# Expert weights fetched in runs of 8 KB, with the channels and rows of each expert dealt to the partitions in another way

## The chip, the cores and the metric

The kernel runs on one core of one Trainium2 chip. The metric is the time of one execution in microseconds (us) on the device: the median of three runs, with their lowest and highest. A profiled execution of the same program gives the trace. Its time includes what lies before the first and after the last instruction; its span does not.

## What is computed

One layer of a decoder trunk for 320 tokens (256 of a prompt, 64 of eight sampled sequences), 1024 channels wide: three mixers, then a mixture of experts, then a gated embedding, and a last norm. The change touches only the mixture of experts, cut here to its core:

```python
g_logits = (t @ w_rg).astype(F32) + b_rg.astype(F32)          # 4 groups
e_logits = jnp.einsum('td,dge->tge', t, w_re) + b_re          # 4 experts in each
...                                                           # best group, two best experts in it
hg = jnp.einsum('td,edf->tef', t, w_gate)                     # 16 experts: 1024 -> 512
hu = jnp.einsum('td,edf->tef', t, w_up)                       #             1024 -> 512
act = jax.nn.silu(hg) * hu * combine[..., None].astype(t.dtype)
return jnp.einsum('tef,efd->td', act, w_down).reshape(b, L, d)  #           512 -> 1024
```

All weights are float32: per expert 2 MB for gate, 2 MB for up and 2 MB for down, 16 experts.

## The kernel before

It is written by hand, engine by engine, with semaphores; the order of each engine's instructions is the order of the code. Before the experts the kernel does the mixers and the router. If no expert has more tokens than the plan holds (the case that runs, `crowded` is 0), the experts are worked on in "sorted" form.

**Tokens are gathered by matmuls.** PE turns the normed activations `h` (channels on partitions) to rows of tokens in six pieces of 512 channels (L2013; `h_bank`, six PSUM banks). ACT copies each piece as float32r into `h_hi` (L961, the copy itself is recorded at the helper's line L683). DVE subtracts: `h_lo` = piece − `h_hi` (`h_rest`, L1407 to 1412), so that `h_hi` + `h_lo` is the full value. For each chunk `c` of 128 channels, `gather` (L2035 to 2047) multiplies `h_hi[:, b, c*128:(c+1)*128]`, and then `h_lo`, by a matrix of zeros and ones `pick_t` (made by DVE, L1453). The product is `h_exp`: 128 channels on partitions, one column for each token's place at an expert.

On ACT the six copies stand ahead of the two exponentials of the router (L964, L966), and DVE's router chain waits for these (L1394). On DVE the six subtractions are spread through the rest of that chain: two before L1419, one before L1429, one before L1433, two before the first `pick_t`. SP waits for `crowded_ready` (L1439) before it fetches the first expert.

**Work goes by items.** There are 4 turns of 5 items, 16 experts in 20 items: 13 items hold 64 places, 7 hold 32. `item_groups(n)`, called `g`, is 2 or 4: an item of 64 places uses the PE array as 2 column tiles of 64, an item of 32 places as 4 tiles of 32. For each of the 8 chunks `k` of 128 channels, tile `p` takes its share of the expert's 512 gate and 512 up columns (L2099 to L2101):

```python
for p in range(g):
    m = MM(bank[0][per * p:per * (p + 1), 0:2 * DE // g], h_exp[i % 2][:, k, first_place(n):first_place(n) + per],
           w_gu[u][:, :, k, DE // g * p:DE // g * (p + 1)], start=k == 0, stop=k == DC - 1)
```

ACT takes the silu (L985), DVE multiplies (`act_s`, L1491), PE turns the product to channels on partitions (L2109), DVE copies it (`act_ft`, L1494), and PE multiplies it with the down weights (L2120, four chunks `k`). The result goes back to the tokens' columns by `scatter` (L2064), which PE does between the chunks of the next item's L2100, as it does the next turn's gathers (L2044, L2046) in the waits around L2109. DVE adds it to `x` (L1477).

**Weights are fetched by SP** in `sorted_experts` (L473 to L492) into two buffers `u`. For each expert SP issues gate and up in halves of four chunks (L485, semaphore `gu_loaded{u}{half}`) and down in one transfer (L489). The gate and up of expert `q` wait for `gu_done` of expert `q-2`, its down for `down_done` of expert `q-2`. PE waits for the first half at `k == 0`, for the second at `k == 4` (L2098), and for down before L2120. After the last expert SP fetches `w_ple_gate` (L471) for the next stage (L2166).

In memory the weights of an expert are rows of 512 (gate, up: 2 KB) or 1024 values (down: 4 KB). In the kernel before, chunk `k` on partition `p` is row `128k + p`, so every partition's piece of a transfer is made of separate rows of 2 or 4 KB.

Of the kernel before, what the change touches and what calls it, by code (L numbers as in the profile page):

```python
# [13 lines left out]
P = 128  # L14
# [33 lines left out]
def build(nc, a, o):  # L48
# [80 lines left out]
    with ExitStack() as ctx:  # L129
# [143 lines left out]
        w_down = [weights[:, u, GU:GU + DOWN].rearrange("p (k n) -> p k n", n=D) for u in range(2)]  # L273
        NI = 4 * CAP + CAP // 2
        h_hi, h_lo = in_place("h_hi", "gates", 0, [P, 3, D]), in_place("h_lo", "gates", 3 * D, [P, 3, D])
        pick_t = in_place("pick_t", "gates", 6 * D, [P, 3, NI])
        silu_s = in_place("silu_s", "gates", 6 * D + 3 * NI, [P, DE // 2], F32)
        act_s = in_place("act_s", "gates", 6 * D + 3 * NI + DE // 2, [P, DE // 2], F32)
# [60 lines left out]
        def _(sp):  # L339
# [133 lines left out]
            def sorted_experts():  # L473


                for q in range(NE):
                    u, item = q % 2, ITEMS * (q // 4) + (0, 1, 2, 4)[q % 4]
                    e = sp.value_load(ids[0:1, item:item + 1], min_val=0, max_val=NE - 1)
                    done = ITEMS * ((q - 2) // 4) + (2, 3, 4, 5)[(q - 2) % 4]
                    if q >= 2:  # L480
                        sp.wait_ge(s("gu_done"), done)
                    for hf in range(2):
                        ks = slice(hf * DC // 2, (hf + 1) * DC // 2)
                        for r, w in enumerate(("w_expert_gate", "w_expert_up")):
                            sp.dma_start(w_gu[u][:, r, ks, :], a[w][0][bass.ds(e, 1)].rearrange(  # L485
                                "e (k p) n -> p (e k) n", p=P)[:, ks, :]).then_inc(s(f"gu_loaded{u}{hf}"), 16)
                    if q >= 2:
                        sp.wait_ge(s("down_done"), done)
                    sp.dma_start(w_down[u], a["w_expert_down"][0][bass.ds(e, 1)].rearrange("e (k p) n -> p (e k) n", p=P)  # L489
                                 ).then_inc(s(f"down_loaded{u}"), 16)  # L490
                sp.wait_ge(s("gu_done"), N_ITEMS - 1)
                ple_gate()  # L492
# [157 lines left out]
        def _(act):  # L650
# [307 lines left out]
            for n_ in range(6):  # L958
                n = BLK[n_ // 2][1]
                act.wait_ge(s("h_tok_turned"), n_ + 1)  # L960
                copy(h_hi[0:n, n_ // 2, 512 * (n_ % 2):512 * (n_ % 2) + 512], h_bank[n_][0:n, :]  # L961
                     ).then_inc(s("h_hi_ready"), 1)
            act.wait_ge(s("router_arg"), 1)
            F(R["gexp"], R["gexp"], ACT.Exp).then_inc(s("router_exp"), 1)  # L964
            act.wait_ge(s("router_arg"), 2)
# [54 lines left out]
        def _(dve):  # L1020
# [385 lines left out]

            def h_rest(n_):  # L1407

                n, f = BLK[n_ // 2][1], slice(512 * (n_ % 2), 512 * (n_ % 2) + 512)
                dve.wait_ge(s("h_hi_ready"), n_ + 1)  # L1410
                TT(h_lo[0:n, n_ // 2, f], h_bank[n_][0:n, :], h_hi[0:n, n_ // 2, f].bitcast(F32), ALU.subtract
                   ).then_inc(s("h_lo_ready"), 1)

            dve.wait_ge(s("moe_const"), 2)
            for n_ in range(2):
# [137 lines left out]
        def _(pe):  # L1553
# [477 lines left out]
            with pe.If(pe.value_load(crowded[:, :], min_val=0, max_val=1) == 0):  # L2031
# [3 lines left out]
                def gather(i, c):  # L2035
# [10 lines left out]
                        m = MM(gather_bank(i, c)[:, 0:ni], h_lo[:, b, f], pick_t[:, b, 0:ni], start=False, stop=b == 2)  # L2046
                    m.then_inc(s("gathered"), 1)

                def scatter(n, half):

                    pe.wait_ge(s("y_lo_ready"), n + 1)
                    pe.wait_ge(s("home_ready"), n + 1)
                    g = item_groups(n)
                    per, js = P // g, DC // g
                    for j in range(js // 2 * half, js // 2 * (half + 1)):
                        done = DC * n + j * g
                        if n == N_ITEMS - 1 and half:
                            pe.wait_ge(s("moe_added"), j * g + g - 4)
                        elif done >= 4:
                            pe.wait_ge(s("down_added"), done + g - 4)  # L2060
                        for y_part in (y_hi, y_lo):
                            for q in range(g):
                                rows_ = slice(per * q, per * (q + 1))
                                m = MM(bank[4 + (j * g + q) % 4][:, 0:T], y_part[rows_, j * P:(j + 1) * P], home_s[rows_, n % 2, :],  # L2064
                                       start=y_part is y_hi, stop=y_part is y_lo)
                                if y_part is y_lo:
                                    m.then_inc(s("spread_done"), 1)
# [19 lines left out]
                for n in range(N_ITEMS):  # L2087
# [8 lines left out]
                    for k in range(DC):  # L2096
                        if k % 4 == 0:
                            pe.wait_ge(s(f"gu_loaded{u}{k // 4}"), 32 * (q // 2 + 1))  # L2098
                        for p in range(g):  # L2099
                            m = MM(bank[0][per * p:per * (p + 1), 0:2 * DE // g], h_exp[i % 2][:, k, first_place(n):first_place(n) + per],  # L2100
                                   w_gu[u][:, :, k, DE // g * p:DE // g * (p + 1)], start=k == 0, stop=k == DC - 1)  # L2101
                        if n and k in (2, 5):
                            scatter(n - 1, k // 5)
                    m.then_inc(s("gu_done"), 1)
# [1 line left out]
                        gather(i + 1, 2 * t)  # L2106
                    pe.wait_ge(s("act_ready"), n + 1)
                    for k in range(4 // g):
                        m = TR(bank[1][:, k * P:(k + 1) * P], act_s[:, k * P:(k + 1) * P], ident[:, :])  # L2109
                    m.then_inc(s("act_turned"), 1)  # L2110
                    if ahead:
                        gather(i + 1, 2 * t + 1)
# [109 lines left out]
```

## Time and profile before

| | us |
|---|---|
| median of 3 runs | 948.44 (947.17 to 950.31) |
| profiled execution, whole | 952.26 |
| its span, first to last instruction | 950.5 |
| PE busy in the span | 864.5 (91%) |
| DVE busy | 408.4 (43%) |
| ACT busy | 213.9 (23%) |
| stage of the experts, start of the first L2100 to start of the last L2120 | 629.4 to 887.7 |

The stage of the experts is some 260 us of the span. A line number is that of the kernel before; copies by ACT's helper all carry L683 and are told apart by their tiles. A float32 matmul leaves two records in the trace, one for each pass, so that 16 matmuls of L2100 read as x32. Where two or four column tiles work side by side, a record's own duration is longer than the distance to the next; distances between groups are what counts.

### The profile page before, as it was taken

The numbers are of one execution on the slowest core, as the hardware profiler recorded it, in microseconds if no ns is written. First come the engines' busy times: TensorE is split into PE (matmuls) and PEld (weight loads), VectorE is DVE, ScalarE is ACT, GpSimd is POOL, SyncE is SP. The second block draws the span as 40 slices with busy tenths as digits, with TensorE's granted clock in tenths as the row PEclk, the third lists the DMA queues.
The fourth block names the chain that finished last, engine by engine and source line by source line (L and its number), as shares of the span: only waits on it lengthen the run. The fifth ranks groups of instructions, "written<-read, shape, count | busy, mean of one in ns | idle before, by whom it ended". The sixth has DMA issues, their size and how long they took to land.

```text
span 950.5 us, 12272 instructions
## 1 busy us (share of the span) xinstructions
PE 864.5 (91%) x4535; PEld 525.2 (55%) x4535; DVE 408.4 (43%) x976; ACT 213.9 (23%) x424; POOL 131.4 (14%) x243
## 2 busy tenths in 40 slices
PE   6699999998689969999989999599999999999695
PEld 4377666765466645756547676564444444433473
DVE  3306664556565243333313413513354453454543
ACT  0211434323232232223250012120111111100233
POOL 4002069998000000000000020000000000000000
PEclk9799999999889979999999999689999999999897
DMA  9323312324852526778673100099999999999601
GB/s 264 91 89 109 137 50 88 111 89 151 274 151 52 176 83 219 223 227 263 227 291 115 44 1 1 0 373 348 396 391 349 391 396 381 395 387 396 225 0 56
DMA packets 108366, 190.36 MB, mean 200 GB/s; under 512 B 9001, under 2 KB 33897, under 8 KB 108295
## 3 DMA queue, kind: packets, MB, share of 16 engines
q1 hardware_dynamic: 103120, 184.40, 54.9%
q0 software_dynamic: 1600, 4.34, 1.6%
q10 hardware_dynamic: 3583, 0.80, 0.5%
q8 instruction: 38, 0.62, 0.3%
q14 instruction: 25, 0.20, 0.1%
HBM read 184.23 MB, written 5.64 MB: 200 GB/s over the span
## 4 chain that ended last, share of the span: by engine, by line
PE 68%; POOL 11%; DVE 8%; ACT 3%; issue 3%; ACTq 3%; SPq 3%; DMA 2%; DVEq 0%; POOLq 0%
PE bank L2100 12%; PE bank L1794 9%; POOL ring L597 7%; PE bank L1621 7%; PE bank L2120 6%; PE bank L1963 6%; PE bank L2166 4%; PE bank L1975 4%; PE bank L2064 3%; POOL proj L600 3%; PE bank L1907 2%; PE bank L1859 2%; PE bank L1877 2%; DMA gate_w<-in_w_in 1%; PE bank L2044 1%
## 5 line engine op out<-in xcount | busy, mean ns | idle before, releaser
L1621 PE MATMUL bank<-scratch,ring 128*128 128x320 f32 x512 | 144.5, 439 | 0.0
L2100 PE MATMUL bank<-weights,h_exp 128*64 128x512 f32 (+1 forms) x864 | 125.6, 488 | 1.2 <-issue 1.2
L1794 PE MATMUL bank<-scratch,gate_w 128*128 128x320 f32 x384 | 114.3, 453 | 11.0 <-DMA gate_w<-in_w_in 10.2
L1621 PEld LDWEIGHTS bank<-scratch,ring 128*128 128x128 f32 x512 | 96.5, 192 | 43.1 <-issue 5.5
L1794 PEld LDWEIGHTS bank<-scratch,gate_w 128*128 128x128 f32 x384 | 74.8, 200 | 44.2 <-DMA gate_w<-in_w_in 11.7
L1477 DVE TENSOR_TENSOR x<-x,bank 128x320 f32<-128x320 f32 x160 | 67.3, 482 | 52.4 <-PE bank L2064 52.4
L2100 PEld LDWEIGHTS bank<-weights,h_exp 128*64 128x64 f32 (+1 forms) x864 | 39.9, 122 | 64.2 <-issue 58.2
L597 POOL TENSOR_SCALAR ring<-scratch,par_w 128x64 f32<-128x64 f32 x120 | 68.8, 600 | 2.9
L2120 PE MATMUL bank<-weights,act_ft 128*64 128x512 f32 (+1 forms) x432 | 61.0, 486 | 0.4 <-DVE act_ft L1494 0.4
L1091 DVE SCALAR_TENSOR_TENSOR proj<-scratch,par_w,proj 128x256 f32<-128x256 f32 x120 | 53.5, 510 | 0.2
L621 POOL MEMSET h_hi<- 64x1024 f32 x1 | 0.9, 946 | 302.3 <-DVE proj L1356 302.3
L683 ACT ACTIVATE gates<-bank 128x320 f32<-128x320 f32 (+3 forms) x38 | 17.5, 477 | 104.1 <-PE bank L1794 99.5
L1859 PE MATMUL bank<-ident,ring 128*128 128x128 f32 x256 | 32.2, 284 | 9.6 <-DVE proj L1269 4.8
L2166 PE MATMUL bank<-scratch,ring 128*128 128x320 f32 x128 | 37.7, 456 | 3.5 <-issue 3.5
L718 ACT ACTIVATE proj<-bank 128x320 f32<-128x320 f32 x32 | 14.0, 436 | 114.9 <-PE bank L1621 114.9
L985 ACT ACTIVATE silu_s<-bank 128x256 f32<-128x256 f32 (+1 forms) x20 | 6.9, 346 | 137.9 <-PE bank L2100 137.9
L1963 PE MATMUL bank<-proj,ring 128*128 128x320 f32 x128 | 36.4, 448 | 1.7 <-DVE att L1309 1.7
L1859 PEld LDWEIGHTS bank<-ident,ring 128*128 128x128 f32 x256 | 29.3, 146 | 14.2 <-DVE proj L1269 5.7
L2120 PEld LDWEIGHTS bank<-weights,act_ft 128*64 128x64 f32 (+1 forms) x432 | 20.3, 122 | 30.1 <-issue 24.6
L1975 PE MATMUL bank<-proj,ring 128*128 128x320 f32 x128 | 35.6, 434 | 1.1 <-DVE proj L1356 1.1
L1269 DVE COPY proj<-bank 128x512 f32<-128x512 f32 x32 | 21.5, 689 | 32.8 <-PE bank L1859 32.5
L1498 DVE TENSOR_TENSOR y_lo<-bank,y_hi 128x512 fp32r<-128x512 f32 (+1 forms) x20 | 12.0, 598 | 50.6 <-ACT y_hi L683 50.6
(354 smaller groups left out, 1128.2 us busy)
## 6 DMA issues: line engine op xcount, KB each, us to landing
weights<-in_w_expert_gate SPq DMA_DIRECT2D x32, 1024.0 KB, 11.0
weights<-in_w_expert_up SPq DMA_DIRECT2D x32, 1024.0 KB, 13.2
weights<-in_w_expert_down SPq DMA_DIRECT2D x16, 2048.0 KB, 16.5
ring<-in_w_in SPq DMA_DIRECT2D x8, 2048.0 KB, 7.7
ring<-in_cache_k SPq DMA_DIRECT2D x64, 256.0 KB, 3.9
ring<-in_cache_v SPq DMA_DIRECT2D x64, 256.0 KB, 3.9
gate_w<-in_w_in SPq DMA_DIRECT2D x24, 512.0 KB, 6.5
ring<-in_w_branch SPq DMA_DIRECT2D x3, 2048.0 KB, 8.8
```

Of the source, the lines that this page charges most:

```text
L597: ch.add(pool.tensor_scalar(tap[:, c, :].rearrange("p (b t) -> p b t", b=NB), src, w, None, ALU.mult))
L600: ch(pool.tensor_tensor(proj[:, TA:TA + WC, SEQ:T], proj[:, TA:TA + WC, SEQ:T], tap, ALU.add))
L1091: ch.add(STT(out, src, w, out, ALU.mult, ALU.add))
L1477: TT(x[:, c, :], x[:, c, :], bank[4 + j % 4][:, 0:T], ALU.add).then_inc(s(name), 1)
L1621: m = MM(bank[b_][:, 0:T], slot(j, DC, GROUP)[:, k, (n % 4) * P:(n % 4 + 1) * P], h[:, k, :], start=k == 0, stop=k == DC - 1)
L1794: m = MM(bank[b_][:, c0:c0 + T], g_w[GW_AT[g]][:, k, :], h[:, k, :], start=k == 0, stop=k == DC - 1)
L1859: m = TR(bank[(0, 1, 5, 6)[j % 4]][:, c * P:(c + 1) * P], slot(u, NPAGE, W)[:, p, c * P:(c + 1) * P], ident[:, :])
L1963: m = MM(bank[4 + n_ % 4][:, 0:T], slot(L % 4, WC, D)[:, k, m_ * P:(m_ + 1) * P], src[:, k, :], start=k == 0, stop=k == WC - 1)
L1975: m = MM(bank[m_][:, 0:T], slot(L % 4, DC, GROUP)[:, k, m_ * P:(m_ + 1) * P], merged[:, k, :], start=k == 0, stop=k == DC - 1)
L2100: m = MM(bank[0][per * p:per * (p + 1), 0:2 * DE // g], h_exp[i % 2][:, k, first_place(n):first_place(n) + per], w_gu[u][:, :, k, DE // g ...
L2120: m = MM(bank[1][per * p:per * (p + 1), 0:D // g], act_ft[:, at_:at_ + per], w_down[u][:, k, D // g * p:D // g * (p + 1)], start=k == 0, s ...
L2166: m = MM(bank[m_ % (4 if m_ < 4 else 2)][:, 0:T], slot(m_ // 4, DC, GROUP)[:, k, (m_ % 4) * P:(m_ % 4 + 1) * P], h[:, k, :], start=i_ == 0 ...
```

## The change

The three layouts move together. Nothing is added, removed or reordered on any engine: each engine has the same instructions in the same order, with other access patterns.

- Gate and up: chunk `k` on partition `p` is now row `8p + k`. A half (four `k`) is four neighbouring rows, 8 KB in one run for each partition.
- The gathered channels must follow: chunk `k` of `h_hi` and `h_lo` must hold channels `8p + k`. ACT's copies and DVE's subtractions read the PSUM piece in its order and write each value 128 values (512 bytes) after the one before, 8 times, then start again one value on (`chunked`). DVE also reads `h_hi` that way. The gathers' own reads stay in one run.
- Down: of the 512 rows, chunk `k = 2g + r` on partition `p` is row `256g + 2p + r`. Two neighbouring rows make a run of 8 KB.
- The activations must follow: the transposes (L2109) take every second column of `act_s` in an item with two tiles. In an item with four tiles the gate and up columns themselves are dealt so (`columns`): a tile reads 128 gate and 128 up values with a step of 2.

```diff
+        def chunked(hs, n_, n):
+            return hs[0:n, n_ // 2, :].rearrange("t (k p) -> t p k", k=DC)[:, 64 * (n_ % 2):64 * (n_ % 2) + 64, :]
...
                             sp.dma_start(w_gu[u][:, r, ks, :], a[w][0][bass.ds(e, 1)].rearrange(
-                                "e (k p) n -> p (e k) n", p=P)[:, ks, :]).then_inc(s(f"gu_loaded{u}{hf}"), 16)
+                                "e (p k) n -> p (e k) n", p=P)[:, ks, :]).then_inc(s(f"gu_loaded{u}{hf}"), 16)
...
-                    sp.dma_start(w_down[u], a["w_expert_down"][0][bass.ds(e, 1)].rearrange("e (k p) n -> p (e k) n", p=P)
+                    sp.dma_start(w_down[u].rearrange("p (g r) n -> p g (r n)", g=2),
+                                 a["w_expert_down"][0][bass.ds(e, 1)].rearrange("e (g p r) n -> p (e g) (r n)", g=2, p=P)
                                  ).then_inc(s(f"down_loaded{u}"), 16)
...
-                copy(h_hi[0:n, n_ // 2, 512 * (n_ % 2):512 * (n_ % 2) + 512], h_bank[n_][0:n, :]
-                     ).then_inc(s("h_hi_ready"), 1)
+                copy(chunked(h_hi, n_, n), h_bank[n_][0:n, :].rearrange("t (p k) -> t p k", k=DC)).then_inc(s("h_hi_ready"), 1)
...
-                TT(h_lo[0:n, n_ // 2, f], h_bank[n_][0:n, :], h_hi[0:n, n_ // 2, f].bitcast(F32), ALU.subtract
-                   ).then_inc(s("h_lo_ready"), 1)
+                TT(chunked(h_lo, n_, n), h_bank[n_][0:n, :].rearrange("t (p k) -> t p k", k=DC),
+                   chunked(h_hi, n_, n).bitcast(F32), ALU.subtract).then_inc(s("h_lo_ready"), 1)
...
+                def columns(g, p):
+                    return slice(256 * p, 256 * (p + 1)) if g == 2 else slice(256 * (p // 2) + p % 2, 256 * (p // 2 + 1), 2)
...
-                                   w_gu[u][:, :, k, DE // g * p:DE // g * (p + 1)], start=k == 0, stop=k == DC - 1)
+                                   w_gu[u][:, :, k, columns(g, p)], start=k == 0, stop=k == DC - 1)
...
-                        m = TR(bank[1][:, k * P:(k + 1) * P], act_s[:, k * P:(k + 1) * P], ident[:, :])
+                        m = TR(bank[1][:, k * P:(k + 1) * P], act_s[:, k:DE // g:4 // g], ident[:, :])
```

## Rows read from the trace of the kernel before

**Rows 1.** The page: its 40 slices of 23.8 us.
```profile
PE   6699999998689969999989999599999999999695
...
PEclk9799999999889979999999999689999999999897
DMA  9323312324852526778673100099999999999601
```

**Rows 2.** Engine time by window: start:end length, busy and count of each engine, clock, DMA.
```profile
680.00:720.00 40.00, 38.79 (x333) 18.38 (x333) 20.50 (x50) 4.77 (x12) 0.00 (x0) 1.00 0.99 374
...
840.00:880.00 40.00, 37.22 (x282) 14.68 (x282) 17.64 (x43) 3.22 (x7) 0.00 (x0) 1.00 1.04 392
```

**Rows 3.** Waits of PE, 629 to 886 us: for whom, us in total, times, longest.
```profile
PE bank L2109 <- DVE act_s L1491: 6.9, 8, 1.0
PE bank L2100 <- issue: 1.2, 1, 1.2
```

**Rows 4.** Timeline: a second half of gate and up issued, and PE at that expert.
```profile
750.77 2.71 SPq L485 DMA_DIRECT2D weights<-in_w_expert_up  x1
...
766.17 2.79 PE L2100 MATMUL bank<-weights,h_exp 128*64 128x512 f32 x12
```

**Rows 5.** L485 between 750 and 751.5 us: issue to landing.
```profile
DMA to landing us min/median/max: 14.2/14.5/14.8
```

**Rows 6.** DMA at 687 to 692 us (gate and up), then 697 to 701 (down).
```profile
DMA packets 975, 1.94 MB, mean 387 GB/s; under 512 B 32, under 2 KB 32, under 8 KB 975
...
DMA packets 414, 1.64 MB, mean 409 GB/s; under 512 B 2, under 2 KB 2, under 8 KB 414
```

**Rows 7.** Timeline of ACT, 600 to 605.5 us: the six copies and the exponentials.
```profile
600.95 0.60 ACT L683 ACTIVATE h_hi<-bank 128x512 fp32r<-128x512 f32 x1 [6.50 <-PE bank L2013]
...
603.45 1.65 ACT L683 ACTIVATE h_hi<-bank 128x512 fp32r<-128x512 f32 x3 [0.26 <-PE bank L2013]
605.00 0.20 ACT L964 ACTIVATE scratch<-scratch 128x12 f32<-128x12 f32 x1
```

**Rows 8.** Timeline of DVE, 606.9 to 617.1 us: the subtractions and their neighbours.
```profile
606.99 1.28 DVE L1411 TENSOR_TENSOR h_lo<-bank,h_hi 128x512 fp32r<-128x512 f32 x2
...
608.42 0.32 DVE L1419 TENSOR_SCALAR rows<-att 16x320 f32<-16x320 f32 x1 [0.15 <-ACT att L683]
...
614.97 0.17 DVE L1436 CAST ids<-bank 1x20 int32<-1x20 f32 x1 [1.49 <-PE bank L2028]
```

**Rows 9.** The chain that ended last, 600 to 621 us: start, us, what.
```profile
610.95 0.59 DVE h_lo L1411
...
615.88 0.56 DVE h_lo L1411
```

**Rows 10.** Timeline at the start of the first item.
```profile
629.24 0.08 DVE L1470 DVE_READ_ACCUMULATOR rows<-bank,home_s 128x1 f32 x1
...
629.42 7.09 PE L2100 MATMUL bank<-weights,h_exp 128*64 128x512 f32 x32 [1.23 <-issue]
```

**Rows 11.** Groups by form: line, shapes, count; busy us, mean ns.
```profile
L683 ACT ACTIVATE y_hi<-bank 128x512 fp32r<-128x512 f32 x13 | 7.8, 597 | 54.2 <-PE bank L2120 54.2
L683 ACT ACTIVATE h_exp<-bank 128x256 f32<-128x256 f32 x24 | 9.2, 383 | 19.9 <-PE bank L2046 19.9
L683 ACT ACTIVATE scratch<-bank 128x240 f32<-128x240 f32 x4 | 1.2, 390 | 0.0
L683 ACT ACTIVATE scratch<-bank 128x128 f32<-128x128 f32 x4 | 1.1, 285 | 0.0
...
L1498 DVE TENSOR_TENSOR y_lo<-bank,y_hi 128x512 fp32r<-128x512 f32 x13 | 9.0, 692 | 40.8 <-ACT y_hi L683 40.8
L1498 DVE TENSOR_TENSOR y_lo<-bank,y_hi 128x256 fp32r<-128x256 f32 x7 | 3.0, 425 | 9.8 <-ACT y_hi L683 9.8
```

**Rows 12.** Timeline of an item with four tiles: three of its eight chunks.
```profile
691.42 1.50 PE L2100 MATMUL bank<-weights,h_exp 128*32 128x256 f32 x24
```

**Rows 13.** L2109, the transposes of `act_s`: duration ns min/median/max.
```profile
L2109 PEld LDWEIGHTS bank<-ident,act_s x33: 137/139/143, 637.5 to 885.4; 128*128 128x128 f32 x33
```

More of the change, by code:

```diff
@@ L1407, in h_rest @@
             def h_rest(n_):
-                n, f = BLK[n_ // 2][1], slice(512 * (n_ % 2), 512 * (n_ % 2) + 512)
+                n = BLK[n_ // 2][1]
                 dve.wait_ge(s("h_hi_ready"), n_ + 1)
-                TT(h_lo[0:n, n_ // 2, f], h_bank[n_][0:n, :], h_hi[0:n, n_ // 2, f].bitcast(F32), ALU.subtract
-                   ).then_inc(s("h_lo_ready"), 1)
+                TT(chunked(h_lo, n_, n), h_bank[n_][0:n, :].rearrange("t (p k) -> t p k", k=DC),
+                   chunked(h_hi, n_, n).bitcast(F32), ALU.subtract).then_inc(s("h_lo_ready"), 1)
             dve.wait_ge(s("moe_const"), 2)
```

## The prediction

> **What bounds the kernel now.** I started from the page's slices [rows 1]. From the 27th slice to the 37th, in the stage of the experts, both PE and DMA stand at 9 tenths. That is the question of this case: two resources look full, the change makes one of them faster, and only a finer view tells which of them ends last. The table by window [rows 2] gives the same picture: PE busy 38.8 and 37.2 of 40 us, DMA share 0.99 and 1.04, some 390 GB/s, clock 1.00, that is 2.4 GHz. A PE that waited for weights would show gaps, so I asked next what PE waits for between 629 and 886 us [rows 3]. It waits for `act_s` of DVE (6.9 us in 8 waits) and 1.2 us before its very first matmul there. No wait for a transfer is listed, in 16 experts.
>
> How close is it? Take the ninth expert. The last piece of its gate and up is issued at 750.77 [rows 4] and lands at most 14.8 us later [rows 5], at 765.6. It is read from chunk 4 on. The group that begins at 766.17 [rows 4] holds chunks 3 to 5 in 12 records and 2.79 us, so chunk 4 begins 4 records later, at 767.1. The slack is 1.5 us. So the transfers are nearly as slow as PE, but they are under it. The 1.2 us before the first matmul is not a wait for weights either: L2100 starts at 629.42, right behind DVE's accumulator read at 629.24 [rows 10], whose result `share_ready` PE waits for.
>
> **The transfers: worked out, then hidden.** Gate and up come in runs of 2 KB at 387 GB/s, down in runs of 4 KB at 409 [rows 6]. On one of 16 engines this is 84.7 and 160.2 ns for a run, so 2 KB more cost 75.5 ns and a run of 8 KB would take about 311 ns: 421 GB/s, an estimate from these two rows. One expert, 4.19 MB and 2.10 MB, goes from 10.84 + 5.13 = 16.0 us to 6.29 MB at 421 = 14.9 us. Over 16 experts that is 16.5 us less transfer. All of it lies under PE, which does not wait for it: I book 0. The bounds are 0 and 16.5. The slack of 1.5 us per expert becomes about 2.5, and since each fetch waits for PE (`gu_done`, `down_done`), the transfers just pause longer. SP's own issue time falls too, and nobody waits for it. The fetch of `w_ple_gate` stands behind the last expert in the queue and lands some 1 us sooner, for a stage that starts when DVE's sums are done: 0.
>
> **ACT's six copies.** This is where the change touches the chain. The same 512 values are written in 64 runs of 8 with a step of 512 bytes. Before the first expert nothing runs in parallel: the six copies run from 600.95 to 605.10, the last three without a gap in 1.65 us, and the exponentials stand behind them [rows 7]; DVE's router waits for these. What does the pattern cost? No row shows such a step. From below: 0 (no row gives a reason for a gain). The nearest row is ACT's copy of 240 values in 8 runs of 30, 390 ns, where the rows of 128 and 256 values in one run (285 and 383 ns) give 371 for 240 [rows 11]: 19 ns for 8 runs, 2.4 ns each. With 64 runs: +0.15 us a copy. From above: each value costs twice what it costs now, (597 − 383) / 256 = 0.84 ns [rows 11], so +0.43 us a copy. I take 0.15. Only the last three copies run back to back, the first three have 0.2 us of slack before PE's next piece, so the chain grows by 3 × 0.15 = **0.45 us**.
>
> **DVE's six subtractions.** Same pattern, and a read in it. Below 0; above again twice the cost of a value, (692 − 425) / 256 = 1.04 ns [rows 11], +0.53 us each. By the nearest row I take about 0, since the run restarts were seen on ACT alone. Four of the six can be felt: the first two end at 608.27, where DVE waits until 608.42 anyway [rows 8]; the third and the fifth are in the chain of waits [rows 9], and the sixth runs right behind the fifth in the 1.28 us of the pair; the fourth lies before a wait of 1.49 us at L1436 [rows 8] and is free up to that.
>
> **PE: columns with a step of 2.** In the 7 items of four tiles L2100 reads every second value. 24 records, three chunks, take 1.50 us [rows 12], so eight chunks take 4.0 us and 7 items 28 us. No row shows a stepped moving operand. Below 0; above, each value twice, +28 us. I take 0, because the step is 8 bytes where the copies have 512; this is the weakest choice here, and it gets a rival. The transposes read `act_s` with step 2 as stationary operand in 13 items. A load takes 139 ns [rows 13]; doubled, 26 of them would be 3.6 us; I take 0, as for the matmuls. The gathers' operands keep their layout: 0.
>
> **The sum:** 0 + 0.45 + 0 + 0 = about +0.5 us, on the profiled execution's 952.26, which stands 3.8 us above the median of the runs. I put it on the median: 948.44 + 0.5 = **948.9 us**, no change that can be measured. A measurement of this kernel can tell about 0.3% (2.8 us) from nothing.
>
> **Rival 1: the stepped copies cost what a value in a new place costs, and the kernel is slower.** If each value costs double: ACT runs six copies of 0.60 + 0.43 without a gap from 600.95, to 607.1 in place of 605.1, +2.0 us. DVE: first two +1.06 less 0.15, third +0.53, fourth hidden, last two +1.06: +2.5. Sum +4.5: **952.9 us**. PE starts the first item late by that much, and nothing later gives it back, as its next waits are few [rows 3]. It decides once a value costs some 0.6 ns more on both engines: with x ns more for each of 512 values ACT's end moves by 3.1x − 0.6 us and DVE's sums by 2.6x − 0.15, together 2.8 at x = 0.63. For it speaks that the chain is bare there, against it that a run restart cost only 2.4 ns. The Trainium skill (Advanced Engine Details and Errata, SBUF Cachelines) speaks against this part of the change: at least two hits on a 16-byte line are needed for full speed, and a new line for each access is penalised. No run here shows it yet. By that rule the copies would go this way, while the step of 2 on PE (two float32 in a line) stays free.
>
> **Rival 2: PE pays for the step of 2.** Up to 28 us, **976 us** at a full doubling; at a tenth of that it already decides. The four tiles read at the same time, which is the reason to fear it. Against: nothing in the trace, which is why it stays.
>
> **Rival 3: faster, because PE does wait for weights outside the profile.** The slack is 1.5 us an expert, and the unprofiled runs are 3.8 us shorter than the profiled one, so PE may be a little faster there and meet the transfers. Then some of the 16.5 us comes back: at half, **940 us**. Against: not one transfer of 16 experts is waited for in the profile [rows 3], even where the DMA share is 1.04 [rows 2]. It needs more than 3 us of such waits.
>
> **Rival 4: the transfers stay as they are,** because a run of 8 KB is cut up again. Then DMA packets and rate don't change and the time follows the copies alone; the number is that of the forecast, so it has no chance of its own.
>
> **How the numbers follow.** Forecast (948.9, by itself 947 to 951.5) 0.52; rival 1 0.31; rival 2 0.09; rival 3 0.08. A small part of rival 1 (0.04, a penalty of half the size) falls within 0.3%. So faster 0.08, same 0.56, slower 0.36. The range takes in forecast and rival 1 with the runs' own spread: 946.3 to 955.0; it leaves out rival 2 at its full size and most of rival 3, under 2 in 10.
>
> **What would show it.** Right: DMA packets of 8 KB and some 420 GB/s while a fetch runs, longer pauses between fetches (DMA share of the stage below 1.0), L2100's groups of 24 records still 1.50 us long, the waits of PE unchanged, the six copies at 0.60 to 0.75 us each, and the first L2100 within 1 us of its place behind L2013. Rival 1: copies near 1.0 us and subtractions near 1.2, and the first L2100 some 4 us later. Rival 2: groups of 24 records longer than 1.65 us. Rival 3: same trace, shorter runs. The forecast is wrong if the median moves by more than 2.8 us either way.

## The result, and the profile after

| | before | after |
|---|---|---|
| median of 20 runs each, us | 948.42 (945.03 to 953.55) | 951.09 (949.57 to 954.05) |
| ratio of the runs, 95% interval | | 1.0031 [1.0017, 1.0046] |
| span of the profiled execution, us | 950.5 | 949.0 |
| DMA packets | 108,366 | 79,694 |
| landing of gate, up, down (median us) | 11.0, 13.2, 16.5 | 10.2, 12.3, 14.0 |

The change makes the kernel 0.31% slower, 2.7 us between the medians, and the interval leaves out 1. The time predicted was 948.9. The measured one is inside the predicted range, and only 0.1 us short of the 2.8 us that the prediction named as the bound of "no change that can be measured". The single profiled execution is even 1.5 us shorter than that of before, so the loss can't be read from the two spans. It has to be read from the stretches.

The page after, with its slices of 23.7 us: PE has its 9 tenths still, and DMA now has some 8s between the 9s [rows 1].

```profile
PE   6699999999689969999989999489999999999695
...
PEclk9799989999989979999999999789999999999898
DMA  9323412324952527778673100098998989989501
```

Engine time by window, columns as in [rows 2]: in these two windows the DMA share is down from 0.99 and 1.04 to 0.88 and 0.92 (over the whole stage from 1.02 to 0.94), while PE is as busy as before.

```profile
680.00:720.00 40.00, 38.67 (x328) 18.36 (x327) 20.41 (x50) 4.83 (x12) 0.00 (x0) 1.00 0.88 356
...
840.00:880.00 40.00, 37.22 (x278) 14.82 (x278) 17.64 (x43) 3.23 (x7) 0.00 (x0) 1.00 0.92 377
```

The transfers, at 700 to 704 us, where the fetches are under way without a pause, 207 of the 230 packets with 8 KB: 424 GB/s where the runs of 2 KB gave 387 and those of 4 KB 409 [rows 6].

```profile
DMA packets 230, 1.70 MB, mean 424 GB/s; under 512 B 23, under 2 KB 23, under 8 KB 23
```

What PE waits for from 629 to 886 us is what it was [rows 3], and no transfer is among it:

```profile
PE bank L2120 <- DVE act_s L1497: 6.9, 8, 1.0
PE bank L2111 <- issue: 1.2, 1, 1.2
```

ACT's timeline (start, us, engine, line, operation): the six copies into `h_hi`, in one row, in place of the six at [rows 7]. Below it the row of line L690 for this tile: duration in ns, lowest/median/highest.

```profile
598.25 5.41 ACT L690 ACTIVATE h_hi<-bank 128x512 fp32r<-128x512 f32 x6 [4.73 <-PE bank L2019]
603.47 0.21 ACT L970 ACTIVATE scratch<-scratch 128x12 f32<-128x12 f32 x1
```

```profile
L690 ACT ACTIVATE h_hi<-bank x6: 1060/1073/1107, 598.3 to 602.6; 128x512 fp32r<-128x512 f32 x4, 64x512 fp32r<-64x512 f32 x2
```

DVE's timeline: the pair of subtractions takes 1.93 us (1.28 before, [rows 8]), one takes 1.00 (0.67), and the small wait before the L1425 of now is gone, since DVE comes later than what it waited for.

```profile
603.72 0.17 DVE L1400 TENSOR_REDUCE scratch<-scratch 128x3 f32<-128x12 f32 x1 [1.82 <-ACT scratch L970]
...
605.47 1.93 DVE L1417 TENSOR_TENSOR h_lo<-bank,h_hi 128x512 fp32r<-128x512 f32 x2
607.32 0.31 DVE L1425 TENSOR_SCALAR rows<-att 16x320 f32<-16x320 f32 x1
...
609.76 1.00 DVE L1417 TENSOR_TENSOR h_lo<-bank,h_hi 128x512 fp32r<-128x512 f32 x1
...
614.18 0.17 DVE L1442 CAST ids<-bank 1x20 int32<-1x20 f32 x1 [1.17 <-PE bank L2034]
...
615.09 1.93 DVE L1417 TENSOR_TENSOR h_lo<-bank,h_hi 64x512 fp32r<-64x512 f32 x2
```

And PE: 24 records of an item with four tiles take 1.56 us instead of 1.50 [rows 12], and a load of `act_s` with its step of 2 has a median of 196 ns instead of 139 [rows 13].

```profile
688.34 1.56 PE L2111 MATMUL bank<-weights,h_exp 128*32 128x256 f32 x24
```

```profile
L2120 PEld LDWEIGHTS bank<-ident,act_s x33: 138/196/219, 636.7 to 885.6; 128*128 128x128 f32 x33
```

To follow the loss I cut each trace at the same instructions. All times in us; "stage" runs from the start of the first L2100 to the start of the last record of L2120.

| | first copy to first exponential | exponential to first `pick_t` | first gather to first L2100 | stage |
|---|---|---|---|---|
| before | 4.05 | 12.09 | 11.01 | 258.25 |
| after | 5.21 | 13.47 | 10.38 | 259.18 |
| difference | +1.16 | +1.38 | −0.63 | +0.93 |

The sum is +2.8 us. That it is close to the 2.7 of the medians means little: the third column is code that nobody touched, and outside the table the first copy starts 2.7 us earlier than before (598.25 against 600.95) and what follows the stage is 1.6 us shorter (61.2 against 62.8). What stands behind these is seen in the first experiments.

### The profile page after: what moved, and what is told of

It reads as the page before. It is cut to its first block, busy times and chain, and to the rows that moved or that the text cites. A ratio compares the mean times of both kernels' runs of the same rounds, so it can differ in the third digit from the quotient of the medians.

```text
span 949.0 us, 12272 instructions
## 1 busy us (share of the span) xinstructions
PE 858.7 (90%) x4535; PEld 521.0 (55%) x4535; DVE 410.0 (43%) x976; ACT 216.3 (23%) x424; POOL 132.1 (14%) x243
## 2 busy tenths in 40 slices
DMA packets 79694, 190.36 MB, mean 201 GB/s; under 512 B 9001, under 2 KB 33897, under 8 KB 67335
## 4 chain that ended last, share of the span: by engine, by line
PE 68%; POOL 11%; DVE 8%; ACT 3%; ACTq 3%; issue 3%; SPq 3%; DMA 2%; DVEq 0%; POOLq 0%
PE bank L2111 12%; PE bank L1800 9%; POOL ring L604 8%; PE bank L1627 7%; PE bank L2131 6%; PE bank L1969 6%; PE bank L2177 4%; PE bank L1981 4%; PE bank L2075 3%; PE bank L1913 2%; POOL proj L607 2%; PE bank L1865 2%; PE bank L1883 2%; DMA gate_w<-in_w_in 1%; SPq L374 1%
## 5 line engine op out<-in xcount | busy, mean ns | idle before, releaser
L1800 PE MATMUL bank<-scratch,gate_w 128*128 128x320 f32 x384 | 112.3, 447 | 10.6 <-DMA gate_w<-in_w_in 9.8
L604 POOL TENSOR_SCALAR ring<-scratch,par_w 128x64 f32<-128x64 f32 x120 | 71.2, 625 | 3.0
L690 ACT ACTIVATE gates<-bank 128x320 f32<-128x320 f32 (+3 forms) x38 | 17.5, 478 | 102.3 <-PE bank L1800 97.6
## 6 DMA issues: line engine op xcount, KB each, us to landing
weights<-in_w_expert_gate SPq DMA_DIRECT2D x32, 1024.0 KB, 10.2
weights<-in_w_expert_up SPq DMA_DIRECT2D x32, 1024.0 KB, 12.3
```

Of the source, the lines that this page charges most:

```text
L604: ch.add(pool.tensor_scalar(tap[:, c, :].rearrange("p (b t) -> p b t", b=NB), src, w, None, ALU.mult))
L1800: m = MM(bank[b_][:, c0:c0 + T], g_w[GW_AT[g]][:, k, :], h[:, k, :], start=k == 0, stop=k == DC - 1)
```

## Experiments

### One part at a time

The transfers alone: before, with both fetches in runs of 8 KB and nothing else. The weights then meet channels and rows that aren't theirs; the amount of work is the same.

```diff
-                                "e (k p) n -> p (e k) n", p=P)[:, ks, :]).then_inc(s(f"gu_loaded{u}{hf}"), 16)
+                                "e (p k) n -> p (e k) n", p=P)[:, ks, :]).then_inc(s(f"gu_loaded{u}{hf}"), 16)
...
-                    sp.dma_start(w_down[u], a["w_expert_down"][0][bass.ds(e, 1)].rearrange("e (k p) n -> p (e k) n", p=P)
+                    sp.dma_start(w_down[u].rearrange("p (g r) n -> p g (r n)", g=2),
+                                 a["w_expert_down"][0][bass.ds(e, 1)].rearrange("e (g p r) n -> p (e g) (r n)", g=2, p=P)
```

> The kernel before with the transfers of the change alone: gate, up and down in runs of 8 KB, every other pattern as before (so the weights meet the wrong channels and rows; the amount of work is that of the kernel before). Theory A (the loss is in the access patterns; transfers lie under PE): same as before within 0.15%, 948 to 949 us, with the DMA share of the experts' stage down from 1.02 to 0.94 and PE's waits unchanged. Theory B (runs of 8 KB cost something by themselves, because longer runs hold up other traffic or the engines' reads): slower, some or all of the 2.7 us. Theory C (the transfers win back something that the patterns lose): faster by 1 us or more.

The patterns alone: the changed kernel with the fetches of before, so again with weights of other channels and rows.

> The changed kernel with the transfers of the kernel before (runs of 2 and 4 KB), so again weights meet wrong channels with the work unchanged. Theory A: as slow as the changed kernel, 951 us (+2.7), since the patterns carry the whole loss. Theory B: back near 948.4. Theory C: slower than the changed kernel, 952 or more.

The down part alone: the runs of 8 KB for down, `columns` and the stepped `act_s`, with gate, up, copies and subtractions as before.

> Only the down rows two by two, with the step of 2 in act_s and in the columns of the items with four tiles; gate, up and the six copies as before. Theory A: PE's share of the loss alone. The stage from the first gate and up matmul to the last down matmul was 0.9 us longer in the changed kernel (257.6 against 256.7), so +0.9 us, 949.3, the copies back at 0.60 and the subtractions at 0.68 us. Rival: if the loss were all in the copies, 948.4.

The gate and up part alone: those two fetches, `chunked` copies and subtractions, with down, L2100 and L2109 as before.

> Only the gate and up rows (8p + k) with the six stepped copies and subtractions; down, act_s and the columns as before. Theory A: the chain's share alone. In the changed kernel the six copies ended 5.4 us after the first began (4.15 before) and the piece from the first exponential's release to the gathers' start was 13.3 us (11.85 before): +2.7 us less what the clock of PE gives or takes, so 950.5 to 951.3. Together with the run of the down rows alone this should add up to the changed kernel.

| 12 runs each, against 35 of before (948.39) | median | ratio, interval | stage | a copy | a subtraction |
|---|---|---|---|---|---|
| transfers only | 949.28 | 1.0004 [0.9984, 1.0023] | 258.25 | 0.60 | 0.68 |
| patterns only | 952.49 | 1.0040 [1.0018, 1.0061] | 259.18 | 1.08 | 1.01 |
| down only | 947.74 | 0.9993 [0.9970, 1.0016] | 259.21 | 0.60 | 0.68 |
| gate and up only | 949.53 | 1.0014 [0.9994, 1.0035] | 258.20 | 1.08 | 1.01 |

The transfers alone change nothing, and the patterns alone carry the whole loss: the interval of their 1.0040 holds the 1.0031 of the full change. They came out 1.5 us above the 951 expected, as Theory C of that run had it (the transfers win something back), but the intervals overlap and the stage is 259.18 us with the long runs and without, so nothing shows such a gain. The stretches split between the two halves: the 0.93 to 0.97 us of the stage come and go with the down part, the long copies with the gate and up part. The times don't show it. Both halves came out below what was expected of them (949.3 for down only, 950.5 to 951.3 for gate and up only), neither is apart from before, and together they stand 0.5 us above it, where patterns only stands 4.1. One reason can be seen in the runs: their granted clocks differ. Its median is 0.963 for down only and 0.959 for gate and up only and for before, but 0.956 for transfers only and 0.957 for patterns only. Over the 35 runs of before, 0.001 less clock goes with some 0.5 us more. Straight lines through the spans of each version, read at a clock of 0.957, give 947.2 us for before, 947.7 for transfers only, 950.1 for patterns only, 949.0 for down only and 948.9 for gate and up only (an estimate). By these the halves add up to 3.4 us, and patterns only is 2.9 above before.

The stage's 0.95 us comes from the step of 2. Groups by form of the version with down only, from 620 to 890 us (busy us, mean ns):

```profile
L2112 PE MATMUL bank<-weights,h_exp 128*64 128x512 f32 x416 | 97.1, 600 | 1.2 <-issue 1.2
L2112 PE MATMUL bank<-weights,h_exp 128*32 128x256 f32 x448 | 29.7, 393 | 0.0
```

The two-tile form, whose columns are still in one run, keeps 600 ns in all four versions; the four-tile form goes from 384 ns (28.5 us, before) to 393. An item with four tiles lasts 9.20 us instead of 9.09, and seven of them make 0.7 us; the rest comes in the last turn, where no gathers lie beside the slower loads of `act_s`.

The versions also show what had muddied the spans. PE turns `h` in six pieces ahead of ACT's copies. Its timeline in the kernel before, then in the version with transfers only:

```profile
593.81 6.00 PE L2004 MATMUL bank<-w_router,scratch 128*128 128x20 f32 x48
599.74 4.70 PE L2013 MATMUL bank<-ident,scratch 128*128 128x128 f32 x24
```

```profile
592.86 4.68 PE L2005 MATMUL bank<-w_router,scratch 128*128 128x20 f32 x48
597.48 2.84 PE L2014 MATMUL bank<-ident,scratch 128*128 128x128 f32 x24
```

The same instructions take 4.70 or 2.84 us. The windows say why: the granted clock from 595 to 604 us is 0.62 in the one and 1.00 in the other.

```profile
595.00:604.00 9.00, 9.00 (x60) 8.82 (x61) 3.79 (x23) 2.34 (x4) 0.00 (x0) 0.62 0.00 0
```

```profile
595.00:604.00 9.00, 5.42 (x55) 5.08 (x55) 5.37 (x33) 3.30 (x8) 0.00 (x0) 1.00 0.00 0
```

A stretch of half clock (1.2 GHz, against 2.4) of some 7 us lies over the pieces in one profile and not in another, though the instructions up to there are the same: in the profiles of before and down only it is there, in those of after, transfers only, patterns only, and gate and up only it is not. It also shifts the third column of the table: half clock lasts for 5.6 us of the first gathers in the profile of before and for 4.2 in that of after. And it decides what the copies cost. At full clock PE delivers the pieces as fast as ACT copies them, and the stretch from first copy to exponential goes from 2.88 us (transfers only) to 5.21 (patterns only): +2.3. At half clock PE is the slower one, a piece each 0.85 us, and the same stretch takes 4.05 with straight copies. Long copies at half clock are in the trace of a later version, the changed kernel with less work for PE behind this point (light after, below). Its clock from 595 to 604 us is 0.63, its six pieces take 4.63 us, and its stretch from first copy to exponential is 5.21 us, as at full clock:

```profile
597.99 4.63 PE L2019 MATMUL bank<-ident,scratch 128*128 128x128 f32 x24
```

```profile
599.20 5.40 ACT L690 ACTIVATE h_hi<-bank 128x512 fp32r<-128x512 f32 x6 [6.56 <-PE bank L2019]
604.40 0.20 ACT L970 ACTIVATE scratch<-scratch 128x12 f32<-128x12 f32 x1
```

So both cases can be set side by side, each with profiles of one clock:

| us | first copy to exponential | exponential to `pick_t` | stage | sum of the differences |
|---|---|---|---|---|
| full clock, transfers only to patterns only | 2.88 to 5.21 | 12.50 to 13.46 | 258.25 to 259.18 | +4.2 |
| half clock, before to light after (stage: before to after) | 4.05 to 5.21 | 12.09 to 13.46 | 258.25 to 259.18 | +3.5 |

The medians of transfers only and patterns only are 3.2 us apart. The unprofiled runs may hold either case, and the interval of the 2.7 us between the first medians, 1.6 to 4.4 us, allows both; the point itself stays below both sums.

### What a step costs, by its size

Before, with each of the six copies and subtractions in another pattern. The same values go to another place, so the tokens' channels arrive in another order. In the first of two versions ACT writes with the step and DVE reads `h_hi` with it; in the second ACT reads PSUM with the step and writes straight, and DVE writes `h_lo` with it.

```diff
+            v = hs[0:n, n_ // 2, 512 * (n_ % 2):512 * (n_ % 2) + 512]
+            st = (2, 4, 8, 128, None, None)[n_]
+            if st:
+                return v.rearrange("t (a b) -> t b a", b=st)
+            r = (2, 4)[n_ - 4]
+            return v.rearrange("t (k p r) -> t p k r", k=4, r=r)
...
-                copy(h_hi[0:n, n_ // 2, 512 * (n_ % 2):512 * (n_ % 2) + 512], h_bank[n_][0:n, :]
+                copy(stepped(h_hi, n_, n), bank_straight(n_, n)).then_inc(s("h_hi_ready"), 1)
```

> The kernel before with another step in each of the six copies (ACT writes h_hi with it, from a straight read of PSUM) and in each subtraction (DVE reads h_hi with it and writes h_lo straight): copies 1 to 4 step 8, 16, 32 and 512 bytes; copy 5 (64 partitions) neighbouring pairs, copy 6 runs of four, both with jumps of 512 bytes and more between. h_hi and h_lo then hold the channels in mixed order, so the experts' sums differ. Theory L (a value that goes to another line of 16 bytes than the one before costs more): steps 16, 32 and 512 and nothing else slow, step 8 and pairs near 0.60 us, 512 at 1.07. Theory S (the size of the step counts): growing from 8 to 512. Theory R (the number of runs counts, not the step): step 512 cheapest of the four at 128 runs of 4, step 8 with 2 runs at 0.60. For DVE's read, Theory L: 0.68 and then up to 1.0; if only its write costs, 0.68 throughout.

> The counterpart: ACT reads PSUM with the steps 8, 16, 32, 512 bytes, pairs, fours, and writes h_hi straight; DVE writes h_lo with the steps and reads straight. Channels mixed as before. Theory L: DVE's write slows from step 16 on, to 1.0 us, with pairs at 0.68; ACT's stepped read of PSUM slows as its write did. If the cost were in SBUF's write side alone, the PSUM reads stay at 0.60.

| 512 values, us | straight | 8 B | 16 B | 32 B | 512 B | pairs | fours |
|---|---|---|---|---|---|---|---|
| ACT writes with the step | 0.597 | 0.631 | 1.090 | 1.141 | 1.103 | 0.638 | 0.577 |
| ACT reads PSUM with the step | 0.597 | 0.597 | 0.597 | 0.597 | 0.597 | 0.590 | 0.590 |
| DVE reads with the step | 0.676 | 0.683 | 1.037 | 1.045 | 1.015 | 0.683 | 0.673 |
| DVE writes with the step | 0.676 | 0.685 | 1.049 | 1.055 | 1.020 | 0.684 | 0.673 |

Each version ran once. The copies with pairs and fours have 64 partitions; straight, such a copy takes 0.59 us. The step of 512 bytes is made of runs of 4 here, where the change has runs of 8; "pairs" and "fours" move 2 or 4 neighbouring values at a time, then jump 512 bytes. DVE's timeline in the first version: a pair with steps of 8 and 16 bytes, then 32, then 512, then pairs and fours.

```profile
604.01 1.64 DVE L1442 TENSOR_TENSOR h_lo<-bank,h_hi 128x512 fp32r<-128x512 f32 x2
...
608.01 1.04 DVE L1442 TENSOR_TENSOR h_lo<-bank,h_hi 128x512 fp32r<-128x512 f32 x1
...
609.58 1.01 DVE L1442 TENSOR_TENSOR h_lo<-bank,h_hi 128x512 fp32r<-128x512 f32 x1
...
613.40 1.28 DVE L1442 TENSOR_TENSOR h_lo<-bank,h_hi 64x512 fp32r<-64x512 f32 x2
```

ACT's copies in the two versions, by form:

```profile
L715 ACT ACTIVATE h_hi<-bank 128x512 fp32r<-128x512 f32 x4 | 3.5, 991 | 6.2 <-PE bank L2044 6.2
```

```profile
L715 ACT ACTIVATE h_hi<-bank 128x512 fp32r<-128x512 f32 x4 | 2.4, 597 | 6.8 <-PE bank L2044 6.8
```

The price jumps once, between 8 and 16 bytes, and stays within a tenth after that. That is Theory L of both expectations, with one miss: it had ACT's stepped read of PSUM slow down as the write did. It is no price for a run that starts again, as in the forecast's 2.4 ns: a step of 16 bytes is 4 long passes, a step of 512 bytes made of 4 values is 128 short ones, and both cost the same. And it is gone on DVE, and down to 0.05 us a copy on ACT, as soon as two neighbouring values are moved together, though 256 pairs jump by 512 bytes or more. This fits one price for each value that has a 16-byte line to itself (no step between 8 and 16 bytes and no pair across two lines was run): (1.103 − 0.597) / 512 = 0.99 ns on ACT, (1.037 − 0.676) / 512 = 0.71 ns on DVE. On DVE a read and a write with the step together cost no more than one of them (1.007 in the changed kernel). This is what the Trainium skill (Advanced Engine Details and Errata, SBUF Cachelines) states, two hits on a 16-byte line for full speed; the runs agree, with these sizes. The Trainium skill (Advanced Engine Details and Errata, PSUM Cachelines) gives 8-byte lines and slow matmuls for any pattern that isn't in one run; here ACT reads PSUM by values 8 to 512 bytes apart at no cost that shows.

### The step on the side that is free

If a stepped read of PSUM is free, the change can have its layout without the price: loop over `k` first, so that ACT and DVE write runs of 64 values and only the bank is read with a step (32 bytes). Everything else is the changed kernel.

```diff
-            return hs[0:n, n_ // 2, :].rearrange("t (k p) -> t p k", k=DC)[:, 64 * (n_ % 2):64 * (n_ % 2) + 64, :]
+            return hs[0:n, n_ // 2, :].rearrange("t (k p) -> t k p", k=DC)[:, :, 64 * (n_ % 2):64 * (n_ % 2) + 64]
...
-                copy(chunked(h_hi, n_, n), h_bank[n_][0:n, :].rearrange("t (p k) -> t p k", k=DC)).then_inc(s("h_hi_ready"), 1)
+                copy(chunked(h_hi, n_, n), h_bank[n_][0:n, :].rearrange("t (p k) -> t k p", k=DC)).then_inc(s("h_hi_ready"), 1)
...
-                TT(chunked(h_lo, n_, n), h_bank[n_][0:n, :].rearrange("t (p k) -> t p k", k=DC),
+                TT(chunked(h_lo, n_, n), h_bank[n_][0:n, :].rearrange("t (p k) -> t k p", k=DC),
```

> The changed kernel with the same layouts, but copies and subtractions walk them in the other order: for each chunk k, 64 values one beside the other. The step (32 bytes) is now on the read of PSUM, where the run with steps showed no cost on ACT (597 ns at each step), and the writes and the read of h_hi go straight. Theory A: copies back at 0.60 and subtractions at 0.68 us, from the first exponential to the first pick_t 12.1 to 12.5 us in place of 13.5, and only the 0.95 us of the stage of the experts left: 949.3 (ratio 1.001). Rival: DVE's read of PSUM costs with a step where ACT's did not; then the subtractions stay at 1.0 and the time near 950.5.

949.92 us (12 runs, 947.41 to 952.87) against 949.43 of before (29 runs of that batch): 1.0005 [0.9982, 1.0027]. The copies and subtractions by form:

```profile
L690 ACT ACTIVATE h_hi<-bank 128x512 fp32r<-128x512 f32 x4 | 2.4, 597 | 7.3 <-PE bank L2019 7.3
...
L1417 DVE TENSOR_TENSOR h_lo<-bank,h_hi 128x512 fp32r<-128x512 f32 x4 | 2.6, 676 | 0.0
```

Both are back at the times of before to the nanosecond, on DVE too. Exponential to `pick_t` takes 12.08 us, as before (12.09, both at half clock); the stage is 259.22, so PE's step of 2 is what is left. With the same layout in memory the long copies and subtractions are gone: their length came from the step on the SBUF side, not from the layout. That the time follows is likely and not shown by the times alone, since the interval of 1.0005 reaches up to 1.0027 and that of the change down to 1.0017.

### Where the faster transfers would count

The theory says that the 16.5 us of faster transfer are real and hidden under PE. To show it, PE has to be made lighter. Both kernels leave out the low parts of the gathers and of the scatter (so `h_lo` and `y_lo` are made and not used); all transfers stay.

```diff
-                        for y_part in (y_hi, y_lo):
+                        for y_part in (y_hi,):
...
-                    for b in range(3):
-                        m = MM(gather_bank(i, c)[:, 0:ni], h_lo[:, b, f], pick_t[:, b, 0:ni], start=False, stop=b == 2)
```

> The kernel before with PE relieved: the experts' results go back to the tokens by their high part alone (scatter without y_lo) and tokens are gathered by h_hi alone, so the small remainders are left out. About 156 scatter and 96 gather matmuls of 0.10 to 0.15 us less, some 25 to 30 us of PE work. Theory A (transfers lie just under PE: 16.0 us an expert, 256 us in all): the stage can't go below some 256 us from its first fetch, so of the 25 to 30 us only a few come off: 940 to 946 us.

> The changed kernel with the same relief. Theory A: now 8 KB runs matter: 14.9 us an expert, 239 us in all, so this one comes out 8 to 14 us below the relieved kernel before. Rival D (8 KB runs move nothing faster in the whole, only packets look shorter): within 3 us of it, above it by the 2.7.

Light before: 943.63 us (7 runs, 942.41 to 947.93), 0.9950 [0.9926, 0.9974] of before (949.87 in that batch). Light after: 934.97 (4 runs, 932.88 to 935.49), 0.9852 [0.9820, 0.9884]. So in this setting the same change gains 8.7 us between the medians, with the loss in the copies inside it, and the runs of the two don't overlap. What PE waits for, 620 to 878 us, light before:

```profile
PE bank L2106 <- DVE act_s L1491: 11.9, 20, 1.0
PE bank L2097 <- DMA weights<-in_w_expert_up: 11.0, 5, 3.5
PE bank L2097 <- DVE rows L1470: 1.2, 1, 1.2
PE bank L2117 <- DMA weights<-in_w_expert_down: 1.1, 1, 1.1
```

And light after, the rows of the same view that stand for `act_s` and for a transfer:

```profile
PE bank L2117 <- DVE act_s L1497: 11.9, 20, 1.0
...
PE bank L2108 <- DMA weights<-in_w_expert_up: 1.1, 1, 1.1
```

12.1 us of waits for weights become 1.1. The windows show both sides: in light before DMA is the bound (share 1.03, 389 GB/s), in light after it moves 409, and PE waits for a transfer once only.

```profile
628.00:876.00 248.00, 226.81 (x1564) 90.26 (x1564) 112.84 (x272) 26.17 (x63) 0.00 (x0) 0.99 1.03 389
```

```profile
628.00:876.00 248.00, 230.27 (x1610) 92.42 (x1606) 116.38 (x281) 29.54 (x71) 0.00 (x0) 1.00 1.00 409
```

The stage goes from 256.78 to 244.61 us, 12.2 less. At the rates of these windows the 100.7 MB of 16 experts take 258.8 and 246.1 us, 12.7 less (an estimate). Note how little light before gained in the stage: it is only 1.5 us shorter than that of before, though PE's busy time from 628 to 888 us fell by 18.6, from 249.5 to 230.9 (25 to 30 expected); most of the rest of its gain stands ahead of the stage, where the first gathers take 7.2 us and not 11.0. The two resources of [rows 1] were both full, with PE ahead by a hair.

### Work taken out of the chain

The chain before the first expert costs whatever stands in it, so I took work out of it without any new layout. ACT makes the last two copies after the exponentials; DVE makes the third and fourth subtraction in its wait ahead of L1436, and the last two after the first `pick_t`; PE waits for `h_lo` only before the matmuls that read it. First with the gate and up part of the change (read of PSUM with the step, no step on PE), then alone.

```diff
-            for n_ in range(6):
+            for n_ in range(4):
...
+            for n_ in range(4, 6):
+                n = BLK[n_ // 2][1]
+                act.wait_ge(s("h_tok_turned"), n_ + 1)
+                copy(h_hi[0:n, n_ // 2, 512 * (n_ % 2):512 * (n_ % 2) + 512], h_bank[n_][0:n, :]
+                     ).then_inc(s("h_hi_ready"), 1)
...
-                pe.wait_ge(s("h_lo_ready"), 6)
...
+                    pe.wait_ge(s("h_lo_ready"), 6)
```

> A try at beating both: gate and up in runs of 8 KB with the stepped read of PSUM, down and its followers as before, and the chain ahead of the first expert reordered: the two exponentials ahead of the fifth copy, the third and fourth subtraction behind the last write of share_r (where DVE waited 1.5 us), the fifth and sixth behind the first pick_t, and the wait for the subtractions moved to the first matmul that reads h_lo. Theory: about 0.6 us off at the third subtraction, about 1 us at the fifth and sixth, 0 to 0.9 at the exponentials: 1.5 to 2.5 us below the kernel before, 946 to 947; the stage of the experts at 258.25 as before. Rival: PE meets the same end because it waits for h_lo instead, no gain.

> The same reordering on the kernel before, transfers and layouts untouched. Theory A (transfers worth nothing here): the same time as the run with gate and up in runs of 8 KB, 946 to 947. If 8 KB runs give something once the chain is shorter, this one is the slower of the two.

With the gate and up part: 947.48 us (12 runs, 940.69 to 950.07), 0.9979 [0.9956, 1.0003]. Alone: 946.99 (12 runs, 943.84 to 949.34), 0.9967 [0.9945, 0.9990]. Both against 949.43 for before. Alone it is faster than before by 0.3%; with the gate and up part the interval holds 1. Runs of 8 KB for gate and up add nothing that can be measured. The changed kernel was not run in that batch; against before it stands at 1.0031. The timelines of the version without them, ACT and then DVE: the exponential now starts 3.0 us behind the first copy (4.05 before), the pair of subtractions fills a wait, and the last pair stands behind `pick_t`.

```profile
601.89 0.60 ACT L683 ACTIVATE h_hi<-bank 128x512 fp32r<-128x512 f32 x1 [0.25 <-PE bank L2020]
602.39 0.20 ACT L964 ACTIVATE scratch<-scratch 128x12 f32<-128x12 f32 x1
602.61 0.20 ACT L966 ACTIVATE scratch<-scratch 128x3 f32<-128x3 f32 x1
602.75 1.13 ACT L683 ACTIVATE h_hi<-bank 64x512 fp32r<-64x512 f32 x2
```

```profile
609.85 1.27 DVE L1416 TENSOR_TENSOR h_lo<-bank,h_hi 128x512 fp32r<-128x512 f32 x2
612.00 0.17 DVE L1441 CAST ids<-bank 1x20 int32<-1x20 f32 x1 [0.88 <-PE bank L2035]
...
613.93 1.20 DVE L1456 TENSOR_TENSOR pick_t<-mask_ssm,att 128x576 fp32r<-128x576 f32 x3 [1.05 <-issue]
615.04 1.27 DVE L1416 TENSOR_TENSOR h_lo<-bank,h_hi 64x512 fp32r<-64x512 f32 x2
```

First copy to `pick_t` is 14.5 us where before has 16.1. The 1.05 us ahead of L1456 is new: it stands at a point where DVE waits for nothing that the profile shows, and it holds most of what moving the last pair should have freed. I didn't follow it further.

## Why the prediction was right and wrong

- **What bounds the kernel: right.** PE in the stage, with transfers just under it. Transfers alone changed neither the stage (258.25 us both) nor the time (1.0004), and in the light pair they became the bound at once.
- **The transfers' size: right for short stretches, some 4 us too large for the stage.** 421 GB/s was worked out, 424 measured over 4 us. Over the 248 us of the light pair it is 389 and 409, so 12.7 us less transfer instead of 16.5, and the stage of the light pair gave back 12.2. The booking at 0 held.
- **ACT's copies: this step failed.** "I take 0.15" a copy, from the row of 240 values in 8 runs. A copy took 1.08 us, 0.48 more, a little above even the upper bound of 0.43; the sign named for the forecast was 0.60 to 0.75. The row measured something else: how often a run starts again. What costs is a value that has a 16-byte line to itself. In the chain the copies gave +1.2 us (PE at half clock) or +2.3 (full clock) against the 0.45 booked. The copies overlap in part (six in 5.41 us, 0.9 us apart), which rival 1 had not seen; its +2.0 lies between the two.
- **DVE's subtractions: this step failed too.** "By the nearest row I take about 0": +0.33 us each, +1.4 in the chain at half clock and +1.0 at full clock, with the fourth hidden as said (the wait at L1436 went from 1.49 to 1.17 us). Rival 1 had +0.53 each. The reason given for 0, that the restarts were seen on ACT alone, was the absence of a row, not a row.
- **PE's step of 2: booked at 0, measured 0.95 us.** Matmuls +4% for a group of 24 records (9 ns of 384 in the mean of a record), loads of `act_s` +57 ns in the median. Small, but a third of the 2.7 us. The prediction's signs had 1.50 us for these 24 records, and 1.56 were measured. A stationary operand with a step is not free at 8 bytes, though copies nearly are.
- **The number: partly luck.** Three terms of the sum that were booked at 0.45 us together come to 3.5 to 4.2 us in the stretches. That the medians are only 2.7 us apart, under the 2.8 named, is within the spread of the runs, whose clock differs, and the range was wide because it took in rival 1. "No change that can be measured" did not hold: the interval is 1.0017 to 1.0046.
- **Which case it was.** Rival 1's mechanism and a small part of rival 2's, together six tenths of rival 1's 4.5 us. Its turning point was 0.63 ns a value on both engines; measured were 0.9 to 1.0 on ACT and 0.65 to 0.7 on DVE. The forecast had put 0.52 on the small price. The rule of the Trainium skill (Advanced Engine Details and Errata, SBUF Cachelines) pointed to rival 1, whose 952.9 us is 1.8 off, and the case was given 0.31. For the unknown price there were a row with restarted runs, the same kind of instruction, and a rule on what the memory does; I weighed the first more.

## What to carry to other kernels

A layout change that helps the transfers is paid where the data is made to follow it: look whether that copy lies in a bare chain, and put the step on the PSUM side with runs of two or more float32 on the SBUF side, which cost 0.05 us a copy at most here. When two resources both read 9 tenths, take one of them away in an experiment: here the same 8 KB runs are worth nothing under PE and 8.7 us once PE is lighter. Cut traces at the same instructions before comparing them, and look at the clock of each stretch, since a stretch of half clock that falls elsewhere moves a span by as much as the change does.

## What was not expected of the hardware

- Step in SBUF, float32: at 8 bytes nothing on DVE and 0.03 us on ACT, then nearly one price at 16, 32 and 512 bytes (ACT 0.597 to 1.09 to 1.14 us, DVE 0.676 to 1.02 to 1.05 for 512 values); for pairs 0.05 us on ACT and none on DVE. A read and a write with the step on DVE cost once, not twice.
- Step in PSUM, float32: no price on ACT's read at 8, 16, 32 or 512 bytes, none on DVE's read at 32.
- The step of 8 bytes that copies hardly feel costs PE 2% to 4% on a moving operand with four column tiles and 40% on a load of 128 columns.
- Copies on ACT overlap: with 1.08 us each the long ones start 0.9 us apart, the straight ones of 0.60 us 0.5 us (transfers only).
- The half-clock stretch near 600 us is there in some profiles and not in others, with the same instructions under it (4.70 against 2.84 us), and changes what the stepped copies cost, +1.2 or +2.3 us. No kernel has two profiles here; but the mean granted clock of the 35 runs of before goes from 0.950 to 0.965.
